# Three attention stages rewritten as one program: split value products over 512 queries, and another order of ScalarE's work

## What is computed

```python
# neighbourhood (NA): 640 of the 1024 keys for a tile of 128 queries
s = jnp.einsum('bhrcd,bhrikd->bhrcik', qg, kg) * (d ** -0.5) + bias
o = einsum(softmax(where(valid, s, NEG)), vg) ; yb = o * silu(zb)
# dilated: three masks in one softmax, written as a weight log(count) per distance
s = einsum(q, k) * Dh ** -0.5 - slope[h] * |pos_q - pos_k|   (+ log multiplicity)
# latent (MLA): no bias
s = (einsum(q_nope, k_nope) + einsum(q_rot, k_rot)) * scale ; o = softmax(s) @ v
```

## Time and profile before

| | |
|---|---|
| Median of 3 runs | 4718.22 us (4712.88 to 4725.39) |
| Profiled execution, its own time | 4719.33 us |
| Its span, first to last instruction | 4717.5 us |
| PE / DVE / POOL / ACT busy | 87% / 47% / 37% / 32% |
| Mean granted clock of TensorE | 0.944 |
| NA stage | 779 to 1002 us |
| Dilated and MLA, layer 0 | 1549 to 1818, 1818 to 2102 us |
| Dilated and MLA, layer 1 | 3290 to 3558, 3558 to 3843 us |

### The profile page before, as it was taken

The page is one execution under the profiler, slowest core; times in us unless marked ns, Lnnn a source line. Parts: engine busy times, 40 slices in busy tenths (PEclk is TensorE's granted clock), DMA queues, the critical chain, the costliest instruction groups (busy, mean ns, idle before and its releaser), DMA issues.

```text
span 4717.5 us, 60741 instructions
## 1 busy us (share of the span) xinstructions
PE 4091.2 (87%) x22152; PEld 3489.1 (74%) x22152; DVE 2223.5 (47%) x4269; ACT 1502.9 (32%) x2417; POOL 1734.4 (37%) x1140
## 2 busy tenths in 40 slices
PE   2999665888689798997899999698998995999998
PEld 1888555777578687886688888576887884888887
DVE  2443585532466565553444443465665543233323
ACT  2221233431233674441211221333773432222221
POOL 2433123531354462002444444453660013444442
PEclk8999888999899899998999999799999997999999
DMA  6665332631135422222123221245323221111111
GB/s 156 195 176 154 100 89 64 137 99 49 72 94 139 105 72 53 48 71 82 63 85 107 77 98 32 85 112 147 79 55 68 48 92 40 41 54 50 49 45 50
DMA packets 300704, 404.65 MB, mean 86 GB/s; under 512 B 45908, under 2 KB 224980, under 8 KB 299860
## 3 DMA queue, kind: packets, MB, share of 16 engines
q1 hardware_dynamic: 293496, 375.60, 28.5%
q10 hardware_dynamic: 6912, 25.17, 1.9%
HBM read 316.23 MB, written 93.63 MB: 87 GB/s over the span
## 4 chain that ended last, share of the span: by engine, by line
PE 67%; issue 8%; DVE 7%; POOL 5%; ACT 3%; DMA 3%; DVEq 2%; SPq 2%; POOLq 1%; ACTq 0%
PE ps L849 10%; PE ps L449 6%; PE ps L450 5%; PE ps L451 5%; PE ps L839 5%; PE ps L1788 5%; PE ps L1789 5%; PE ps L1790 5%; PE ps L1804 5%; PE ps L1806 4%; PE ps L1805 4%; POOL rs L738 2%; PE ps L885 1%; PE ps L886 1%; PE ps L1475 1%
## 5 line engine op out<-in xcount | busy, mean ns | idle before, releaser
L404 POOL TENSOR_TENSOR WL<-RAW,WH 128x1024 fp32r<-128x1024 f32 x226 | 556.2, 2473 | 1194.9 <-ACT WH L386 1184.6
L449 PE MATMUL ps<-WH,XTh 128*128 128x512 f32 (+1 forms) x1536 | 611.6, 398 | 47.7 <-POOL XTl L498 25.1
L451 PE MATMUL ps<-WL,XTh 128*128 128x512 f32 (+1 forms) x1536 | 601.0, 391 | 0.0
L450 PE MATMUL ps<-WH,XTl 128*128 128x512 f32 (+1 forms) x1536 | 600.9, 391 | 0.0
L386 ACT ACTIVATE WH<-RAW 128x1024 fp32r<-128x1024 f32 x226 | 234.5, 1063 | 826.1 <-PE ps L1806 347.7
L1824 DVE TENSOR_TENSOR X<-ps,X 128x512 f32<-128x512 f32 x512 | 349.1, 689 | 254.1 <-PE ps L1806 253.1
L1788 PE MATMUL ps<-XTh,WH 128*128 128x512 f32 x1024 | 401.7, 392 | 18.4 <-POOL XTl L498 18.4
L1804 PE MATMUL ps<-WH,Hh 128*128 128x512 f32 x1024 | 401.2, 392 | 4.0 <-DVE X L1824 3.3
L1789 PE MATMUL ps<-XTl,WH 128*128 128x512 f32 x1024 | 400.6, 391 | 0.0
L1790 PE MATMUL ps<-XTh,WL 128*128 128x512 f32 x1024 | 400.4, 391 | 0.0
L1805 PE MATMUL ps<-WH,Hl 128*128 128x512 f32 x1024 | 398.7, 389 | 0.0
(11 more groups left out here) (196 smaller groups left out, 7680.5 us busy)
## 6 DMA issues: line engine op xcount, KB each, us to landing
RAW<-w_all SPq DMA_DIRECT2D x232, 512.0 KB, 3.7
WM<-w_mod ACTq DMA_DIRECT2D x48, 512.0 KB, 4.3
WM<-w_mod SPq DMA_DIRECT2D x48, 512.0 KB, 4.1
QS<-QA_d SPq DMA_DIRECT2D x24, 512.0 KB, 3.8
KHs<-KA_d SPq DMA_DIRECT2D x48, 256.0 KB, 6.1
KLs<-KA_d SPq DMA_DIRECT2D x48, 256.0 KB, 6.8
VS<-VA_d SPq DMA_DIRECT2D x20, 512.0 KB, 7.2
X<-x SPq DMA_DIRECT2D x2, 4096.0 KB, 13.9
```

The costliest lines, as they stand in the source:

```text
L404: e.tensor_tensor(w_low(n), w_raw(n), w_high(n).bitcast(F32), ALU.subtract).then_inc(w_ready, 1)
L449: e.matmul(bank, a, w, start=(kc == 0), stop=False)
L450: e.matmul(bank, b, w, start=False, stop=False)
L451: j = e.matmul(bank, a, l, start=False, stop=(kc == K - 1))
```

## The change

The three stages share one program, `heads`, with a function for each engine (`heads_sp`, `heads_pe`, `heads_act`, `heads_dve`, `heads_pool`).

- The transposed probabilities are kept as a high part (fp32r, rounded by ACT: `high`) and a low part (made by DVE: `low`), four units (512 queries, a **group** G) side by side; the values also as a high and a low part, 64 columns each, side by side in VHL (ACT `value_high`, POOL `value_low`, once per head). `values(G)` takes VHL as the weights and 512 queries as the columns: two fp32r products for each tile of keys (8, NA 6), in three parts spread over the next three units. PTh and PTl are cleared once where NA's group has tiles that a unit does not fill.
- The result lies turned (64 high rows above 64 low rows, 512 queries). ACT copies it out (`copy_out`), PE turns it back and adds the two halves in one step with twoI, two unit matrices on top of each other (`turn_back`), and DVE makes the output of four tiles at once.
- ACT takes all of the transposed tiles, in two halves per unit, where it took one and DVE the other. Its order is high(u), exps(u+1), and in the dilated stage then `distances(u+2)`, which is the old `scaled`, for three units in four. For the units with u % 4 == 3 POOL makes that product itself (a tensor_scalar in `far`) ahead of its addition.
- The maximum comes negated from its own instruction, so L1384 and L1488 go. In NA and the dilated stage the scores are written negated and the exponential has scale -1, in place.
- Loads: a head's slot is reloaded when the scores of the head two before are done; values are loaded once per pair of heads, the slopes once per stage.

Cut to its core (the tile declarations, the semaphores, `Heads` with its counts, and the removed bodies that are shown above are left out; `ge(e, s, v)` waits for s to reach v if v is positive):

```diff
-                def scaled(u):
-                    if na:
-                        return
-                    h, t = divmod(u, T)
-                    if t == 0:
-                        head_loaded(e, a, h, LD)
-                    e.wait_ge(s["max"], a.c(u - 1))
-                    e.activation(BI[:, u % 2, :], DIST[:, t, :], ACT.Copy, scale=slp[:, h % 2, 0:1]).then_inc(s["comb"], 1)
-                    if t == T - 1:
-                        e.drain().then_inc(s["bused"], 1)
-
-                def exps(u):
-                    o = u % 2
-                    e.wait_ge(s["max"], a.c(u + 1))
-                    e.wait_ge(s["tr"], a.c(u - 1))
-                    e.wait_ge(s["out"], a.c(u - 3))
-                    e.activation(Pb[:, o, 0:W], Sb[:, o, 0:W], ACT.Exp, bias=nmx[:, o:o + 1],
-                                 accum_out=rl[:, u % 4:u % 4 + 1]).then_inc(s["exp"], 1)
-
-                scaled(0)
-                scaled(1)
-                exps(0)
-                for u in range(a.n):
-                    if u + 2 < a.n:
-                        scaled(u + 2)
-                    if u + 1 < a.n:
-                        exps(u + 1)
-                    copy_turned(who, a, u, PTr, tiles, 0)
...
+        def heads_sp(who, a):
+            e, s = who.e, a.s
+            for h in range(8):
+                slot, p = h % 2, h // 2
+                if h >= 2:
+                    e.wait_ge(s["full"], a.u0 + 8 * (h - 1))
+                ld = a.loaded(h)[0]
+                if a.kind == "mla":
+                    e.dma_start(QMh[:, slot, :].bitcast(F32), QM_d[h, 0]).then_inc(ld, 16)
+                    e.dma_start(QMl[:, slot, :].bitcast(F32), QM_d[h, 1]).then_inc(ld, 16)
+                    e.dma_start(KMh[0:NOPE, slot, :].bitcast(F32), KM_d[h, 0]).then_inc(ld, 16)
+                    e.dma_start(KMl[0:NOPE, slot, :].bitcast(F32), KM_d[h, 1]).then_inc(ld, 16)
+                if a.kind == "dil":
+                    load64(e, QA_d, KA_d, h, slot, QSd, KHd, KLd, ld)
+                if a.kind == "na":
+                    load64(e, QB_d, KB_d, h, slot, QSn, KHn, KLn, ld)
+                    if h >= 2:
+                        e.wait_ge(s["bias"], a.own + 8 * (h - 1))
+                    for a2 in range(2):
+                        e.dma_start(NAB[64 * a2:64 * a2 + 64, slot, :].rearrange("p (a b) -> p a b", b=GRID_W),
+                                    NAB_d[h][:, 1 - a2:1 - a2 + NA_E, GRID_W - 1:2 * GRID_W - 1]).then_inc(ld, 16)
+                if h % 2 == 0:
+                    vld = a.v_loaded(p)[0]
+                    if p >= 2:
+                        e.wait_ge(s["vlo"], a.h0 + 2 * p - 2)
+                    load_v(e, {"na": VB_d, "dil": VA_d, "mla": VM_d}[a.kind], p, p % 2, a.VS, vld)
+                    if a.narrow:
+                        if p >= 2:
+                            e.wait_ge(s["out"], a.g0 + 4 * p - 4)
+                        load_v(e, ZB_d, p, p % 2, ZSn, vld)
...
+        def heads_pe(who, a):
+            e, s = who.e, a.s
+            half = a.W // 2
+            scores_read = s["exp"] if a.kind == "mla" else s["max"]
+
+            def scores(u):
+                h, t = divmod(u, T)
+                if t == 0:
+                    e.wait_ge(*a.loaded(h))
+                ge(e, scores_read, a.u0 + u - 1)
+                k0 = a.tiles(t)[0] * P
+                for b in range(2):
+                    keys = slice(k0 + b * half, k0 + (b + 1) * half)
+                    bank = ps[:, 2 * (u % 2) + b, 0:half]
+                    if a.kind == "mla":
+                        e.matmul(bank, QMh[:, h % 2, tok(t)], KMh[:, h % 2, keys], start=True, stop=False)
+                        e.matmul(bank, QMh[:, h % 2, tok(t)], KMl[:, h % 2, keys], start=False, stop=False)
+                        j = e.matmul(bank, QMl[:, h % 2, tok(t)], KMh[:, h % 2, keys], start=False, stop=True)
+                    else:
+                        Q, KH, KL = (QSn, KHn, KLn) if a.narrow else (QSd, KHd, KLd)
+                        e.matmul(bank, Q[:, h % 2, tok(t)], KH[:, h % 2, keys], start=True, stop=False)
+                        j = e.matmul(bank, Q[:, h % 2, tok(t)], KL[:, h % 2, keys], start=False, stop=True)
+                j.then_inc(s["full"], 1)
+
+            def turn(u):
+                n = len(a.tiles(u % T))
+                e.wait_ge(s["exp"], a.u0 + u + 1)
+                for b in range(2):
+                    ge(e, s["lo"], 2 * (a.u0 + u) - 1 + b)
+                    for k in range(4 * b, min(4 * b + 4, n)):
+                        j = e.transpose(ps[:, 4 + b, (k % 4) * P:(k % 4) * P + P], a.P[:, u % 2, k * P:k * P + P], ident[:])
+                    j.then_inc(s["tr"], 1)
+
+            def values(G, part):
+                h, g = divmod(G, 2)
+                keys = a.group(g)
+                if part == 0:
+                    e.wait_ge(s["lo"], 8 * (a.g0 + G + 1))
+                    e.wait_ge(s["vlo"], a.h0 + h + 1)
+                    ge(e, s["ot_copied"], a.g0 + G)
+                third = (len(keys) + 2) // 3
+                for n in range(third * part, min(third * part + third, len(keys))):
+                    v = a.VHL[:, h % 2, keys[n], :]
+                    e.matmul(ps[:, 6, :], v, a.PTh[:, G % 2, n, :], start=(n == 0), stop=False)
+                    j = e.matmul(ps[:, 6, :], v, a.PTl[:, G % 2, n, :], start=False, stop=(n == len(keys) - 1))
+                if part == 2:
+                    j.then_inc(s["ot"], 1)
+
+            def turn_back(G):
+                e.wait_ge(s["ot_copied"], a.g0 + G + 1)
+                ge(e, s["out"], a.g0 + G)
+                for r in range(4):
+                    j = e.matmul(ps[:, 7, 64 * r:64 * r + 64], a.OT[:, G % 2, r * P:r * P + P], twoI[:], start=True, stop=True)
+                j.then_inc(s["back"], 1)
+
+            scores(0)
+            for u in range(N_UNITS + 4):
+                G, r = divmod(u, 4)
+                if u + 1 < N_UNITS:
+                    scores(u + 1)
+                if u < N_UNITS:
+                    turn(u)
+                if G >= 1 and r < 3:
+                    values(G - 1, r)
+                if G >= 1 and r == 3:
+                    turn_back(G - 1)
...
+        def heads_act(who, a):
+            e, s = who.e, a.s
+
+            def exps(u):
+                e.wait_ge(s["max"], a.u0 + u + 1)
+                to = a.P[:, u % 2, 0:a.W]
+                if a.kind == "mla":
+                    ge(e, s["tr"], 2 * (a.u0 + u) - 2)
+                    e.activation(to, ps[:, 2 * (u % 2):2 * (u % 2) + 2, :].rearrange("p b c -> p (b c)"), ACT.Exp,
+                                 bias=mx[:, u % 4:u % 4 + 1], accum_out=rl[:, u % 16:u % 16 + 1]).then_inc(s["exp"], 1)
+                else:
+                    e.activation(to, to, ACT.Exp, bias=mx[:, u % 4:u % 4 + 1], scale=-1.0,
+                                 accum_out=rl[:, u % 16:u % 16 + 1]).then_inc(s["exp"], 1)
+
+            def distances(u):
+                h, t = divmod(u, T)
+                ge(e, s["max"], a.u0 + u - 1)
+                e.activation(BId[:, u % 2, :], DIST[:, t, :], ACT.Copy, scale=SL[:, h:h + 1]).then_inc(s["dist"], 1)
+
+            def high(u):
+                G, r = divmod(u, 4)
+                t = u % T
+                n, n0 = len(a.tiles(t)), a.at(t)
+                if r == 0:
+                    ge(e, s["ot"], a.g0 + G - 1)
+                for b in range(2):
+                    k0, k1 = 4 * b, min(4 * b + 4, n)
+                    e.wait_ge(s["tr"], 2 * (a.u0 + u) + 1 + b)
+                    e.activation(a.PTh[:, G % 2, n0 + k0:n0 + k1, r * P:r * P + P],
+                                 ps[:, 4 + b, 0:(k1 - k0) * P].rearrange("p (k q) -> p k q", q=P), ACT.Copy).then_inc(s["hi"], 1)
+
+            def copy_out(G):
+                e.wait_ge(s["ot"], a.g0 + G + 1)
+                ge(e, s["back"], a.g0 + G - 1)
+                e.activation(a.OT[:, G % 2, :], ps[:, 6, :], ACT.Copy).then_inc(s["ot_copied"], 1)
+
+            def value_high(h):
+                e.wait_ge(*a.v_loaded(h // 2))
+                ge(e, s["ot"], a.g0 + 2 * h - 2)
+                o0 = 64 * (h % 2)
+                e.activation(a.VHL[:, h % 2, :, 0:64], a.VS[:, h // 2 % 2, :, o0:o0 + 64], ACT.Copy).then_inc(s["vhi"], 1)
+
+            value_high(0)
+            if a.kind == "dil":
+                distances(0)
+                distances(1)
+            exps(0)
+            for u in range(N_UNITS + 4):
+                G, r = divmod(u, 4)
+                if G >= 1 and r == 3:
+                    copy_out(G - 1)
+                if u < N_UNITS:
+                    high(u)
+                if u + 1 < N_UNITS:
+                    exps(u + 1)
+                if a.kind == "dil" and u % 4 != 1 and u + 2 < N_UNITS:
+                    distances(u + 2)
+                if u % T == 5 and u + 3 < N_UNITS:
+                    value_high(u // T + 1)
...
+        def heads_dve(who, a):
+            e, s = who.e, a.s
+
```

(140 more changed lines are left out.)

265 lines of the change are left out of this document (46 added, 219 removed).

## The result

The changed kernel takes 4912.4 us (median of 4 runs, 4909.64 to 4918.57), the kernel before 4719.2 (4 runs): a ratio of 1.041 [1.0394, 1.0426], 193 us slower. The profiled execution has a span of 4910.8 us and a mean granted clock of 0.916, where it was 0.944.

What follows compares the result with a forecast made beforehand. PE was taken to set the pace. Dilated +243, MLA -73 and NA -17 made +153 on a span of 4717.5, 4871 us after own time and median correction; range 4828 to 4920, about 8 in 10.

Steps and rivals of the forecast that it cites:

- the closed loop over one unit: Dilated stage: distances(u+2) behind exps(u+1) close a loop over one unit, not two; with tail +121.6 us a stage, two +243.
- The loop's length: Dilated stage: maximum through exponential, distances and POOL's addition to the next maximum, 6.36 us, 46 times.
- T: Dilated stage: POOL's tensor_scalar product in units with u % 4 == 3, taken as 1.3 us, making a 3.83 us step.
- the rival with 2.4: Dilated stage: POOL's product as slow as a sum of two, 2.4 us; +35, 4906 us; chance 0.12.
- Tail of a dilated stage: Dilated stage, work after the last exponential: 9.2 us against 7.0, +2.2.
- lower-clock rival: Dilated stages: PE falls to its lower clock; 6 us in short steps, +4 in the tail, 4891 us; chance 0.17.
- Start of a dilated stage: Dilated stage: first value rounding ahead of the first distances, +0.6 us.
- MLA: MLA stages: no such loop, PE at 3.51 us a unit against 4.12; -36.4 a stage, two -73.
- The rival in which MLA and NA gain nothing: MLA and NA: ACT's chain is 4.1 us and not 3.1, +73 + 17, 4961 us; chance 0.05.
- NA: NA stage: 2.45 us a unit, 3.4 a head at seven stops, start -1.5, tail +3.1; -17 us.
- The faster rival: Dilated stages: the loop doesn't close, ACT's 3.4 us bounds a unit; -132, 4586 us; chance 0.06.
- The break-even: Dilated stage: the whole change breaks even where a unit costs 0.73 more than before, 4.5 us.

Runs made afterwards that it cites:

- kernels 1 and 2: 1: changed kernel with ACT's distances(u+2) ahead of high(u) and exps(u+1), 4647.6 us; 2: kernel before with its distances behind exps(u+1), nothing else changed, 5058.4 us.
- Kernel 7: Changed kernel, its own order, with value_low moved behind the bias of a head's third unit: 4913.2 us.
- kernel 9: kernel 5 with value_low, in NA alone, behind the bias of a head's third unit, the first value_low included: 4555.8 us.
- kernel 1: Changed kernel with ACT's distances(u+2) ahead of high(u) and exps(u+1): 4647.6 us.
- kernel 5: Changed kernel with distances first in ACT's queue and all products on ACT, none on GpSimd: 4578.0 us.
- kernel 4: Changed kernel with ACT's distances(u+2) between high(u) and exps(u+1): 4731.5 us.
- kernel 3: Changed kernel with ACT's order distances(u+2), exps(u+1), high(u): 4881.8 us.

## Why the prediction was right, point by point

The forecast was 4871 us, slower; it is 4912, inside the range and 41 over the forecast. The step that carried it, the closed loop over one unit, is shown from both sides by kernels 1 and 2. The sizes were off in terms that partly cancel, and there was luck in it: the upper end of the range was 4920, and the dilated stages and NA alone were 60 us over their forecasts. Without MLA, 19 us better than forecast, the time would have been 4931.

- **The loop's length**: 6.36 from the earlier trace rows, measured 6.21 to 6.25 in the steady state and 6.26 in the mean of the 46 (one near the start is 7.8): -4.6 us a stage.
- **T, the price of GpSimd's product**: this is the mis-sized term. I took 1.3 us between 0.9 and 2.3; it is 2.85, beyond the upper bound, and beyond the rival with 2.4. Groups by form of the kernel after:

```profile
L1536 POOL TENSOR_TENSOR BId<-BId,TB 128x1024 f32<-128x1024 f32 x128 | 303.9, 2375 | 344.8 <-ACT BId L1408 340.1
...
L1534 POOL TENSOR_SCALAR BId<-DIST,SL 128x1024 f32<-128x1024 f32 x32 | 91.1, 2846 | 0.0
```

  The bound was drawn from a one-input select of 128 columns, 0.292 us, stretched by columns; that row was another operation. The short step is 5.34 and not 3.83: +24.2 a stage, +48 in all, more than the whole miss. The Trainium skill's GPSIMD Engine Reference (4.1 Engine selection) puts GpSimd against VectorE: about twice as slow with two inputs, roughly at line rate with one. The first half agrees with this trace (its sum 2.37 us, VectorE's sum of two inputs with its minimum, L1464, 1.22 over the same 1024 columns); the second does not: the one-input product is 20% slower than the two-input sum of the same size.
- **Tail of a dilated stage**: +2.2 forecast, +5.7 measured (8.5 to 14.2 us from the last maximum). The timeline of PE at its end:

```profile
1949.26 0.63 PE L1368 MATMUL ps<-PTld,VHLd 128*128 128x512 f32 x1
1949.69 0.63 PE L1367 MATMUL ps<-PThd,VHLd 128*128 128x512 f32 x1
1950.11 0.63 PE L1368 MATMUL ps<-PTld,VHLd 128*128 128x512 f32 x1
...
1953.41 0.40 PE L1368 MATMUL ps<-PTld,VHLd 128*128 128x512 f32 x1
1953.65 0.40 PE L1367 MATMUL ps<-PThd,VHLd 128*128 128x512 f32 x1
```

  Twelve of the 16 products start about 0.43 us apart, the level of 1.2 GHz, the last ones 0.24, that of 2.4; in layer 1 five do, and the tail is +5.0. So 12 x 0.19 = 2.3 of the 3.5 us that were missed in layer 0 are the lower level. That part of the lower-clock rival was right; it had +4. Its other part, 6 us in the short steps, can't be seen: with T at 2.85 the step is long enough to cover PE. The stage's granted clock is 0.79, and PE pauses in each unit for up to 2.9 us. TensorE: Matmul & The Clock Gate of the Trainium skill (Part 1), an idle array falls to half its clock, agrees.
- **Start of a dilated stage**: +0.6 forecast, +1.5 measured.
- **MLA**: -36.4 forecast, -45.7 measured (layer 0). Four units of PE are 13.65 us (transposes begin at 2060.25, 2063.44, 2066.61, 2070.25, 2073.90) and not 14.04; 8 transposes take 0.80 us here (2060.25 to 2061.05), I had 0.90 from the earlier trace rows. From the first maximum to the last the stage gave 46.3 us, 7.7 more than forecast, all of it in the new unit: 213.4 / 63 = 3.39 us where I had 3.51. The tail gave back 3.3 and not 2.2. The stage also starts 2.7 us sooner, which the forecast lacked: before, PE's first scores were released by the load of the values, 12.8 us after the last output of the stage ahead; after, the values have a semaphore of their own, and PE was released by the last load of keys, 10.1 us after. The rival in which MLA and NA gain nothing is refuted: PE is full there, as said.
- **NA**: -17 forecast, -4.1 measured. Three pieces. From first to last maximum NA went from 197.1 to 185.9 us, -11 and not -19 (the prediction's 198.05 ran to the negation after the last maximum). The stop at a head is where it was put:

```profile
788.66 0.63 PE L1344 MATMUL ps<-KHn,QSn 128*128 128x320 f32 x1 [20.72 <-DMA NAB<-NAB_d]
...
792.16 0.63 ACT L1431 ACTIVATE VHLn<-VSn 128x512 fp32r<-128x512 f32 x1 [23.81 <-DMA ZSn<-ZB_d]
792.94 1.26 POOL L1515 TENSOR_TENSOR VHLn<-VSn,VHLn 128x512 fp32r<-128x512 f32 x1 [18.69 <-ACT VHLn L1431]
...
794.15 2.61 POOL L1525 TENSOR_TENSOR NAB<-NAB,CMK 128x1152 f32<-128x1152 f32 x1
...
913.32 1.30 POOL L1515 TENSOR_TENSOR VHLn<-VSn,VHLn 128x512 fp32r<-128x512 f32 x1 [3.22 <-ACT VHLn L1431]
...
914.57 2.65 POOL L1525 TENSOR_TENSOR NAB<-NAB,CMK 128x1152 f32<-128x1152 f32 x1
...
919.02 0.82 DVE L1464 CUSTOM_DVE_ANT_0 Pn<-ps,BIn 128x640 f32<-128x640 f32 x1 [4.04 <-issue]
...
920.89 1.33 PE L1354 MATMUL ps<-ident,Pn 128*128 128x128 f32 x5 [3.56 <-DVE PTln L1478]
```

  These are two stretches of NA's timeline after, all engines: its start, and a change of head. The maximum before 919.02 was at 912.66: a step of 6.36 us. What I had not counted follows it: PE, idle for 3.56 us, does 5 transposes in 1.33 us instead of 0.77, and the maximum after next comes 4.25 us after its predecessor. Steps differ within a group of four units (1.8 to 3.3 us even undisturbed), so groups have to be compared: the first four units of a head take 14.5 us, the last four 9.6. A head's stop therefore costs 4.9 us, where I had 3.4, and the steady unit, 2.40, was forecast well with 2.45: 63 x 2.40 + 7 x 4.9 = 185.5. Kernel 7 takes 3.0 us a head away by the place of `value_low` alone.
  The start: I wrote -1.5 for V behind the table; it is +2.5 (24.3 to 26.8 us from the first load to the first maximum). The table did come sooner, 16.8 us after the first load where it took 19.7, and released PE at 788.66, but POOL's queue begins with `value_low(0)`, which waits for the values, and the mask began at 794.15. I had followed the transfer to its end but not to who waits for it; kernel 9 shows this term. The tail took 4.6 more, for 3.1.
- **The faster rival** (4586) had 3.4 us a dilated unit with ACT as the bound. With the loop open, kernel 1 is 62 us above that, because T makes POOL's step 5.37; with T gone (kernel 5) it is 4578 and ACT is the bound at 3.33. The condition was put right, its price needed T.
- **The break-even**: "The loop would have to lose 1.9 of its mean 5.7" is a slip. 1.9 is the way back to the old unit of 3.8; to the break-even at 4.5 it is 1.2. The price itself held: kernel 4 has 4.55 us a unit and ends 0.3% over the kernel before.

Together, against +153: dilated +47, MLA -19, NA +13, other stages -1: 40 more, the measured +193.

## What to carry to other kernels

Before an instruction is moved on an in-order engine, write down the loop that it closes: from a unit's result through every queue back to the next unit's, with how many units the loop spans; one more unit of lead (distances first) was worth 265 us, where the whole change with it gains 72. Splitting one result over two engines (ACT's high part, DVE's low part) adds such an edge, so an order that was free before has to be checked again. An operation that is seldom issued in a new place (a product on GpSimd, a rounding once a head) is priced from a row of its own kind or left as wide as the ignorance is, and the same edit is to be judged under the bound that will hold once the larger fault is mended.

## What the runs showed of the hardware

- GpSimd's product of 128x1024 float32 with one scalar a partition takes 2.85 us, its sum of two tiles of that size 2.37; VectorE's sum of two with a running minimum, 1.22.
- PE's granted clock went with the length of the pauses: 0.82 between 1600 and 1900 us of the changed kernel, with pauses of up to 2.9 us (its PE busy for 206 of 300 us); 1.00 in kernel 5's dilated stage, with PE busy for 173 of 190; and 1.00 in kernel 3's too, where PE is busy for only 169 of 230 us but no pause is over 1.4. A single pause of 3.56 us was followed by 5 transposes in 1.33 us instead of 0.77, and by slower ones in the next unit too (1.23 at 924.79).
- Work that runs at the lower level can hide: in the dilated loop 8 transposes took 1.95 us in some units and 1.09 in others, and the steps were 6.22 and 6.24.
